# GpSimd in place of ScalarE and VectorE splits the chunk of weights that lands during each attention

## What is computed

```python
for layer in range(DEPTH):                      # DEPTH = 2
    h = rms_norm(x, norm_g[layer])
    p = h @ w_in[layer]
    c_q, c_kv, k_r, gate_a, dil_qkv, gate_b = jnp.split(p, split_points, axis=-1)
    a = mla_attention(c_q, c_kv, k_r, ...) * jax.nn.silu(gate_a)
    b = dilated_attention(dil_qkv, cos_d, sin_d) * jax.nn.silu(gate_b)
    x = x + jnp.concatenate([a, b], axis=-1) @ w_out[layer]
```

## Time and profile before

| | |
|---|---|
| median of three runs | 2206.28 us (2205.87 to 2206.8) |
| the profiled execution's own time | 2205.55 us |
| its span, first to last instruction | 2203.8 us |
| TensorE busy | 2126.2 us, 96% of the span |
| VectorE busy | 1171.2 us, 53% |
| ScalarE busy | 776.3 us, 35% |
| GpSimd busy | 39.9 us, 2% |
| mean granted TensorE clock | 0.988 of full speed |
| loads of weights, `WS<-in_w_in` | 1024 KB each, 5.4 us from issue to landing |

### The profile page before, as it was taken

The page is one execution under the profiler, slowest core; times in us unless marked ns, Lnnn a source line. Parts: engine busy times, 40 slices in busy tenths (PEclk is TensorE's granted clock), DMA queues, the critical chain, the costliest instruction groups (busy, mean ns, idle before and its releaser), DMA issues.

```text
span 2203.8 us, 28271 instructions
## 1 busy us (share of the span) xinstructions
PE 2126.2 (96%) x11693; PEld 1756.1 (80%) x11693; DVE 1171.2 (53%) x1589; ACT 776.3 (35%) x1229; POOL 39.9 (2%) x75
## 2 busy tenths in 40 slices
PE   6999999999999999999999998999999989999997
PEld 5888878678888887688888886787788867888886
DVE  4655556656555557654444446685643446333334
ACT  3252334533242525543222224354633233222223
POOL 0101000000101000000000001000000000000000
PEclk9999999999999999999999999999999999999998
DMA  4423212112313222113232224233032221333221
GB/s 151 120 66 96 77 58 79 39 50 84 116 40 115 68 77 69 40 58 95 95 95 95 96 97 143 77 115 115 21 96 96 96 95 61 104 96 101 95 96 39
DMA packets 157280, 188.49 MB, mean 86 GB/s; under 512 B 4018, under 2 KB 147700, under 8 KB 157044
## 3 DMA queue, kind: packets, MB, share of 16 engines
q1 hardware_dynamic: 152256, 174.34, 25.0%
q0 software_dynamic: 4464, 12.47, 1.8%
q10 hardware_dynamic: 452, 0.15, 0.0%
HBM read 181.68 MB, written 7.36 MB: 86 GB/s over the span
## 4 chain that ended last, share of the span: by engine, by line
PE 88%; DVE 7%; ACT 3%; issue 2%; DMA 1%; SPq 0%; DVEq 0%; ACTq 0%
PE PS L881 26%; PE PS L883 26%; PE PS L882 26%; PE PS L967 4%; PE PS L1008 2%; PE PS L979 2%; PE PS L1093 1%; DVE WL L1745 1%; DVE TMP L1997 1%; ACT PR L1379 1%; DMA ARENA<-in_x 1%; ACT PR L1376 0%; DVE PS L1853 0%; DVE X L2009 0%; PE PS L931 0%
## 5 line engine op out<-in xcount | busy, mean ns | idle before, releaser
L881 PE MATMUL PS<-UH,WH 128*128 128x512 f32 x1712 | 675.5, 395 | 20.7 <-DVE UL L1798 10.2
L883 PE MATMUL PS<-UH,WL 128*128 128x512 f32 x1712 | 669.7, 391 | 0.0
L882 PE MATMUL PS<-UL,WH 128*128 128x512 f32 x1712 | 669.7, 391 | 0.0
L1306 ACT ACTIVATE WH<-WS 128x2048 fp32r<-128x2048 f32 x103 | 197.3, 1916 | 621.9 <-PE PS L883 621.9
L881 PEld LDWEIGHTS PS<-UH,WH 128*128 128x128 f32 x1712 | 323.7, 189 | 92.9 <-issue 19.1
L883 PEld LDWEIGHTS PS<-UH,WL 128*128 128x128 f32 x1712 | 323.4, 189 | 68.6
L882 PEld LDWEIGHTS PS<-UL,WH 128*128 128x128 f32 x1712 | 323.7, 189 | 66.4 <-issue 0.7
L1745 DVE TENSOR_TENSOR WL<-WS,WH 128x2048 fp32r<-128x2048 f32 x103 | 235.8, 2289 | 229.9 <-ACT WH L1306 229.7
L2023 DVE TENSOR_TENSOR WL<-WS,WH 128x2048 fp32r<-128x2048 f32 x44 | 100.7, 2288 | 149.3 <-ACT WH L1462 149.3
L1462 ACT ACTIVATE WH<-WS 128x2048 fp32r<-128x2048 f32 x44 | 84.4, 1917 | 260.0 <-PE PS L883 260.0
L881 PE MATMUL PS<-HH,WH 128*128 128x512 f32 x352 | 136.9, 389 | 0.0
(11 more groups left out here) (279 smaller groups left out, 2674.0 us busy)
## 6 DMA issues: line engine op xcount, KB each, us to landing
WS<-in_ffn_w SPq DMA_DIRECT2D x66, 1024.0 KB, 5.2
WS<-in_w_in SPq DMA_DIRECT2D x64, 1024.0 KB, 5.4
WS<-in_w_out SPq DMA_DIRECT2D x8, 1024.0 KB, 5.1
WS<-in_w_gate SPq DMA_DIRECT2D x8, 1024.0 KB, 5.4
WS<-in_w_attn_out SPq DMA_DIRECT2D x4, 1024.0 KB, 5.1
WS<-in_w_lru_out SPq DMA_DIRECT2D x4, 1024.0 KB, 5.1
WS<-in_w_o SPq DMA_DIRECT2D x4, 1024.0 KB, 5.1
bias_skewed<-bias_rows POOLq DMA_DIRECT2D x1, 3072.0 KB, 13.8
```

Of the source, the lines that this page charges most:

```text
L881: nc.tensor.matmul(dst, sh, mh, start=start, stop=False, skip_group_check=True)
L882: nc.tensor.matmul(dst, sh, ml, start=False, stop=False, skip_group_check=True)
L883: return nc.tensor.matmul(dst, sl, mh, start=False, stop=stop, skip_group_check=True)
L1306: nc.scalar.activation(WH[:, c % 2, 0:kt * n], WS[:, c % 2, 0:kt * n], ACT.Copy).then_inc(w_hi, 1)
```

## The change

In the seven attentions the quarters are taken out of ScalarE's and VectorE's programs. In GpSimd's program a new function `split_in(name)` splits the same chunks, each whole: one copy WS -> WH (128x2048, with rounding) and one subtraction WS - WH -> WL. It waits for the load, for the product of chunk c - 2, and for the counts `w_hi` and `w_split` of the chunks before, and adds to the same semaphores as the quarters did. It stands behind GpSimd's DMAs for the values of each dilated attention, behind those of the second half also for the mla attention of that layer, and at the end of GpSimd's program for swa. At the end of each attention ScalarE waits for `w_hi` and VectorE for `w_split` of chunk c0 + 2. Nine chunks are concerned: four in dil, four in mla, one in swa.

```diff
--- before.py
+++ after.py
@@ gpsimd
+            def split_in(name):
+
+                c0 = pl.chunk[filler_of[name]]
+                for c in range(c0 + (1 if name[0] == "mla" else 2), c0 + 3):
+                    pool.wait_ge(landed[c % 2], 16 * (c // 2 + 1))
+                    pool.wait_ge(acc_ready, pl.acc[pl.chunks[c - 2][3]])
+                    pool.wait_ge(w_hi, c)
+                    nc.gpsimd.tensor_copy(WH[:, c % 2, :], WS[:, c % 2, :]).then_inc(w_hi, 1)
+                    pool.wait_ge(w_hi, c + 1)
+                    pool.wait_ge(w_split, c)
+                    nc.gpsimd.tensor_tensor(WL[:, c % 2, :], WS[:, c % 2, :], WH[:, c % 2, :].bitcast(F32),
+                                            ALU.subtract).then_inc(w_split, 1)
...
                     pool.wait_ge(v0_in, 16 * 12 * (n + 1))
+                    split_in(("dil", L, hh))
+                split_in(("mla", L))
...
             pool.dma_start(BIAS, bass.AP(BSKEW.tensor, 127, [[383, P], [P * 384, QH], [1, 256]])).then_inc(bias_in, 16)
+            split_in(("swa",))
@@ scalar
-            def hi_part(c, i):
-
-                if i == 0:
-                    act.wait_ge(landed[c % 2], 16 * (c // 2 + 1))
-                    act.wait_ge(acc_ready, pl.acc[pl.chunks[c - 2][3]])
-                part = slice(i * 512, (i + 1) * 512)
-                ins = nc.scalar.activation(WH[:, c % 2, part], WS[:, c % 2, part], ACT.Copy)
-                if i == 3:
-                    ins.then_inc(w_hi, 1)
...
-                    c, i = pl.chunk[filler_of[name]] + (1 if mla else 2), n - n0 - 1
-                    if 0 <= i < (8 if mla else 4):
-                        hi_part(c + i // 4, i % 4)
...
+                act.wait_ge(w_hi, pl.chunk[filler_of[name]] + 3)
@@ vector
-            def lo_part(c, i):
-
-                if i == 0:
-                    dve.wait_ge(w_hi, c + 1)
-                part = slice(i * 512, (i + 1) * 512)
-                ins = tt(WL[:, c % 2, part], WS[:, c % 2, part], WH[:, c % 2, part].bitcast(F32), ALU.subtract)
-                if i == 3:
-                    ins.then_inc(w_split, 1)
...
-                    c, i = pl.chunk[filler_of[name]] + (1 if mla else 2), n - n0 - 4
-                    if 0 <= i < (8 if mla else 4):
-                        lo_part(c + i // 4, i % 4)
...
+                dve.wait_ge(w_split, pl.chunk[filler_of[name]] + 3)
```

## The result

The changed kernel takes 2210.3 us (median of 17 runs, 2209.27 to 2212.83), the kernel before 2206.28 us beside it (17 runs, 2202.51 to 2207.05). The ratio is 1.0021, 95% interval 1.0014 to 1.0027: slower by 0.21% (the two medians themselves lie 4.0 us apart, 0.18%). The prediction was 2204.5 us, a little faster, with a range of 2189 to 2209. The profiled execution of the changed kernel took 2209.77 us, its span is 2208.0 us and its mean granted clock 0.983.

A forecast was written before the change was run, and what follows sets the result against it. TensorE bounds the kernel (88% of the chain that ended last). Removing the quarters gains 15.6 us, GpSimd's reads ahead of mla cost 13.8 us: -1.8 us, carried to the median of 2206.28 us gives 2204.5 us, range 2189 to 2209.

The forecast's parts named there:

- the clock behind the stall: Ahead of mla: after TensorE's 4.7 us stall the granted clock falls and costs a further 2.7 us a layer.
- the last item of a dilated attention: End of each dilated attention: 0.35 us of the 3.23 us surplus stays as latency from scores to transposes.
- the loss behind the subtraction: Ahead of mla: a VectorE instruction with two SBUF inputs waits for GpSimd's whole subtraction, 3.7 us as middle value.
- Part 1, dilated attentions: Quarters leaving ScalarE and VectorE remove TensorE's stalls: 2.9 us for each of four dilated attentions, 11.6 us (10 to 12.8).
- Part 1, mla and swa: Without quarters, mla rounds at head group ends go from 4.22 to 3.85 us, 1.5 us in all; swa gains 2.5 us.
- Part 2: GpSimd's copy (1.83 to 3.7 us) and subtraction (1.83 to 5.5, taken 3.7) for each of nine chunks are in time.
- rival (d): GpSimd's splits come too late, the product behind the attention waits and stalls only change places: about 2206 us; chance 0.03.
- Part 3: Ahead of mla: GpSimd's reads hold up VectorE's rotary products, 4.2 us plus 2.7 us of clock a layer, 13.8 in all.
- Rival (a): The forecast: GpSimd's reads hold VectorE up ahead of mla; 2204.5 us, own range 2195.3 to 2208.7; chance 0.57.
- part 1: In the attentions: taking the quarters off ScalarE and VectorE gains 15.6 us in all, bounds 13.5 and 17.4.
- Rival (b): No contention between GpSimd and VectorE, only the gains in the attentions remain: 2190.7 us (2189 to 2193); chance 0.29.
- rival (c): Slower: contention ahead of mla with a subtraction above 6.5 us; with 8 us it is 2213.7 us; chance 0.11.

The follow-up runs named there:

- The kernel with the changed tail: Late form, with VectorE copying both halves of the transposes in the last but one item of dil and swa attentions: 2187.87 us, 0.9919 against the kernel before.
- two repeat kernels: Kernel before, GpSimd untouched, VectorE's last rotary instruction ahead of mla's scores repeated four times or twice: 2225.89 us (1.0092) and 2220.62 us (1.0061).
- late form: Changed kernel plus one wait: in mla GpSimd's first split starts only after VectorE's last tile ahead of the attention; 2192.47 us, 0.9945 against the kernel before.
- kernel with copies: Late form plus three extra GpSimd copies WS to WH at the old place, beside the rotary products: 2204.19 us, 0.9993 against the kernel before.
- kernel with two repeats: Kernel before, with VectorE's last rotary instruction ahead of mla's scores made two more times: 2220.62 us, 1.0061 against the kernel before.

## Why the prediction missed, by its own steps

The mechanism of the forecast was right in all three parts. What failed are sizes of its sum: the clock behind the stall (2.7 us a layer forecast, 4.1 and 4.2 measured), the last item of a dilated attention (0.35 us left over, 0.96 measured) and the loss behind the subtraction (3.7 us forecast, 4.28 measured).

**Part 1, dilated attentions: right cause, one term mis-sized.** The quarters did set the four stalls, and all four distances became 3.14 us. The surplus of 3.23 us is gone but for the last item, and there the step failed. I left 0.35 us of latency, by counting the last item's own scores, maxima and exponentials. What stays is 0.31 us for VectorE's copy plus 0.51 us for ScalarE's, with the transposes cut in two pieces: 0.96 us of surplus. I had overlooked that ScalarE owes a copy for the item before and has the last item's exponentials queued ahead of it. 2.26 us were gained for each attention where 2.9 were forecast, 9.0 instead of 11.6 in all. The kernel with the changed tail took that copy away and the wait with it.

**Part 1, mla and swa: right.** 1.5 us forecast for mla, 1.55 measured; in the trace after, the round at the end of a head group takes 3.84 us instead of 4.22. For swa 2.5 us forecast, 2.75 measured.

**Part 2: right.** The splits were in time everywhere, against rival (d): the first runs from 135.35 to 141.87 us, the attention lasts until 158.7 us, and the chunk is wanted one product later. The copy took 1.89 us, near the lower end of its bounds. The subtraction took 4.54 us where I took 3.7, the middle of a wide bound. The Trainium skill, GPSIMD Engine Reference, section Performance versus the Vector engine, has 4497 ns for a two-input operation on 2048 fp32 elements; the trace agrees to 1%, with 4.54 us.

**Part 3: right cause, both sizes too small.** VectorE was held as described, with SQ behind the copy and one rotary product behind the whole subtraction. The stall grew by 4.7 us instead of 4.2: 0.40 us behind the copy and 4.28 behind the subtraction, where I had 0.5 and 3.7. That is 1.0 us in two layers. The larger miss is the clock. I had taken 2.7 us a layer from two other places, where it was back some 6 and 5 us after TensorE began again. Here it was back after 9.4 us and cost 4.1 and 4.2 us: 2.9 us more in two layers. The two repeat kernels show the same place giving 4.55 and 5.15 us.

**The sum.** Forecast -1.8 us on the profiled execution. The three misses, 2.6 (dilated tail), 1.0 (stall) and 2.9 (clock), less 0.25 (swa) give -1.8 + 6.25 = +4.4; +4.2 stands in the ledger, whose stretches outside the forecast (-1.3 and +1.1) make up the difference. Rival (a), the forecast's mechanism, held, and yet its upper bound, 2208.7 us, was passed. Its price of 18.0 us was not: 17.7 us were paid, with the stall's loss below its upper end of 6.0 us and the clock above its own of 3.0, which I had put hardly beyond two readings. But I had set the price against the middle of part 1, 15.6 us, and 13.3 were gained, a little less even than part 1's lower bound of 13.5. With that bound the upper end would have been 2206.3 - 13.5 + 18.0 = 2210.8 us, and the range would have held the result. Rival (b) named what is to be had without the collision: 2190.7 forecast, 2192.5 measured in the late form. The threshold of rival (c), a subtraction above 6.5 us, was wrong for the same reasons: with 4.1 us of clock and 13.3 us of gains, 2 x (0.5 + s + 4.1) = 13.3 + 4.4 is reached at s = 4.3 us, and the subtraction took 4.54. So the case that I gave 0.11 began 0.6 us above my own forecast's term, and the result, 4.0 us slower, lies at its edge. Another slip is in the chances: for a time below 2201.9 us at the forecast's clock price the subtraction has to stay under 2.4 us, not 3.

**Where the gain went.** 13.3 us were gained in the attentions and 17.7 given back in the two stretches ahead of mla, 9.3 of that because VectorE was held up and 8.4 by the clock behind it.

## What to carry to other kernels

When work goes to GpSimd, look not for a place where GpSimd is idle but for one where VectorE has no instruction with two SBUF inputs on the critical path, and write the wait that keeps it there: here one wait turned +0.21% into -0.55%. Where it must overlap, cut GpSimd's instruction short, since VectorE waits for the whole of the one that runs. Price a stall of TensorE as its length plus what the clock takes behind it, from a spread of readings and not from the nearest two. When a range is made, join the upper end of the price to the lower end of the gain. Cost the last item of a pipeline by all that is queued on each engine it needs.

## What the runs showed of the hardware that I had not expected

- Each of the two engines holds up the other, and the profile puts the waiting into the duration: GpSimd's subtraction shows 5.46 us behind VectorE's SQ and 4.54 alone.
- A copy on GpSimd from f32 to fp32r, one tensor in, costs 1.89 us for 128x2048, near a memset's 1.83, while the subtraction costs 2.4 times that.
- The price of the clock behind a stall ahead of mla, by stall: 2.14 us gave 0 or 3.0 us, 2.94 gave 3.0, 3.00 gave 4.55, 5.17 gave 4.1 and 5.52 gave 5.15. TensorE worked at 1.2 GHz for about 7 us behind the stall of 2.94 and about 9.4 behind that of 5.17. The stalls of 2.94 and 3.00 us differ by 1.5 us because the clock came back later: a share of 0.62 puts the return at about 402.8 in the kernel with copies, 8.4 us behind its first scores, and a share of 0.69 puts it at about 409.2 in the kernel with two repeats, 10.5 us behind them. Why it stayed low longer there stays open. The two rows, copies first:

```profile
402.00:403.00 1.00, 1.00 (x4) 0.76 (x4) 0.00 (x0) 0.00 (x0) 0.00 (x0) 0.62 0.69 196
...
408.00:410.00 2.00, 1.89 (x6) 1.16 (x4) 0.00 (x0) 0.07 (x1) 0.00 (x0) 0.69 0.00 0
```
